# Two fused transformer blocks on one core: where the token's scale of the norm ahead of the experts is applied, and how a score's mask and maximum are formed

## The reference

```python
def rms_norm(x, g):
    y = x * lax.rsqrt(jnp.mean(x * x, axis=-1, keepdims=True) + EPS)
    return y * g

def peer(xn, peer_w_q, peer_sub_keys, peer_u, peer_v):
    qh = (xt @ peer_w_q).reshape(T, 8, 2, 128)                # queries
    sub = jnp.einsum("thpc,hpnc->thpn", qh, peer_sub_keys)    # against 2 x 128 keys a head
    v1, i1 = lax.top_k(sub[:, :, 0], 16)
    v2, i2 = lax.top_k(sub[:, :, 1], 16)
    cand = v1[..., :, None] + v2[..., None, :]                # 256 candidates a head
    vals, cidx = lax.top_k(cand, 16)
    gates = jax.nn.softmax(vals, axis=-1)
    # for the 16 experts of each head and token: h = xn . u, then gelu(h) * gate, then the sum with v
    ...

x = x + mixed @ w_out
x = x + peer(rms_norm(x, norm2_g), peer_w_q, peer_sub_keys, peer_u, peer_v)
```

## Time and profile before

| | us |
|---|---|
| median of 3 runs | 3203.68 (3203.49 to 3206.08) |
| the profiled execution | 3204.81 |
| its span | 3203.0 |
| TensorE busy in the span | 3185.0 |
| VectorE busy | 2226.0 |
| ScalarE busy | 1555.5 |

### The profile page before, as it was taken

How to read it: one execution, slowest core, us unless ns; L and a number is a source line. 1 busy time by engine, 2 the same in 40 slices (tenths; PEclk the granted TensorE clock), 3 DMA queues, 4 the chain that set the end, 5 groups by cost and what they waited for, 6 DMA issues and landing times.

```text
span 3203.0 us, 42378 instructions
## 1 busy us (share of the span) xinstructions
PE 3185.0 (99%) x17362; PEld 2707.6 (85%) x17362; DVE 2226.0 (69%) x3055; ACT 1555.5 (49%) x1998; POOL 13.7 (0%) x29
## 2 busy tenths in 40 slices
PE   9999999999999999999999999999999999999999
PEld 8888888888888888887888888888888788888887
DVE  6775556677577567766568997766687787865564
ACT  4564444555355455546544555455443344444353
POOL 0000000000000000000000000000000000000000
PEclk9999999999999999999999999999999999999999
DMA  7456665656665666653555666666666665556665
GB/s 252 154 162 218 211 211 180 210 191 191 191 190 190 193 188 192 205 170 111 190 154 171 217 216 189 188 183 224 190 190 212 203 200 173 188 184 192 194 184 171
DMA packets 175825, 610.61 MB, mean 191 GB/s; under 512 B 19201, under 2 KB 27553, under 8 KB 174736
## 3 DMA queue, kind: packets, MB, share of 16 engines
q1 hardware_dynamic: 173648, 599.93, 60.0%
q0 software_dynamic: 1984, 7.99, 0.8%
HBM read 597.36 MB, written 10.49 MB: 190 GB/s over the span
## 4 chain that ended last, share of the span: by engine, by line
PE 97%; DVE 2%; ACT 1%; issue 0%; DMA 0%; SPq 0%; ACTq 0%; DVEq 0%
PE PS L1194 29%; PE PS L1211 16%; PE PS L1213 16%; PE PS L1212 16%; PE PS L1191 15%; PE PS L1414 1%; PE PS L1427 1%; PE PS L1293 1%; DVE LO L1749 0%; PE PS L1247 0%; PE PS L1326 0%; ACT UN L1506 0%; ACT HI L1436 0%; PE PS L1305 0%; PE PS L1223 0%
## 5 line engine op out<-in xcount | busy, mean ns | idle before, releaser
L1749 DVE TENSOR_TENSOR LO<-RAW,HI 128x1024 fp32r<-128x1024 f32 (+1 forms) x1096 | 1325.1, 1218 | 698.0 <-ACT HI L1436 694.7
L1436 ACT ACTIVATE HI<-RAW 128x1024 fp32r<-128x1024 f32 (+1 forms) x1096 | 1148.3, 1054 | 1044.6 <-PE PS L1213 732.5
L1194 PE MATMUL PS<-XX,HI 128*128 128x512 f32 x4032 | 968.4, 391 | 0.0
L1194 PEld LDWEIGHTS PS<-XX,HI 128*128 128x128 f32 x4032 | 739.4, 188 | 145.1 <-issue 2.4
L1211 PE MATMUL PS<-HI,FH 128*128 128x512 f32 x1760 | 692.0, 393 | 1.7 <-DVE LO L1749 1.7
L1213 PE MATMUL PS<-HI,FL 128*128 128x512 f32 x1760 | 685.8, 390 | 0.0
L1212 PE MATMUL PS<-LO,FH 128*128 128x512 f32 x1760 | 684.7, 389 | 0.0
L1191 PEld LDWEIGHTS PS<-XX,LO 128*128 128x128 f32 x4032 | 520.2, 191 | 21.1 <-issue 1.0
L1191 PE MATMUL PS<-XX,LO 128*128 128x256 f32 x4032 | 536.8, 284 | 0.0
L1213 PEld LDWEIGHTS PS<-HI,FL 128*128 128x128 f32 x1760 | 330.3, 188 | 70.1
L1211 PEld LDWEIGHTS PS<-HI,FH 128*128 128x128 f32 x1760 | 330.3, 188 | 69.1 <-DVE LO L1749 2.2
(11 more groups left out here) (286 smaller groups left out, 1667.7 us busy)
## 6 DMA issues: line engine op xcount, KB each, us to landing
RAW<-in_peer_ut SPq DMA_DIRECT2D x256, 512.0 KB, 4.1
RAW<-in_peer_v SPq DMA_DIRECT2D x256, 512.0 KB, 4.2
RAW<-in_ffn_w_up SPq DMA_DIRECT2D x176, 512.0 KB, 4.2
RAW<-in_w_in SPq DMA_DIRECT2D x88, 512.0 KB, 4.3
RAW<-in_ffn_w_down SPq DMA_DIRECT2D x88, 512.0 KB, 4.2
RAW<-in_w_in_c SPq DMA_DIRECT2D x48, 512.0 KB, 3.7
RAW<-in_w_mix_out SPq DMA_DIRECT2D x32, 512.0 KB, 4.0
RAW<-in_w_in_2c SPq DMA_DIRECT2D x32, 512.0 KB, 3.7
```

Source lines behind the costliest of these rows:

```text
L1194: m = e.matmul(o, hi[:, k, x], XX[:, 4 * u + k, :, :].rearrange("p h s -> p (h s)"), start=first and k == 0, stop=last and k == 3, skip_gr ...
L1436: return e.activation(dst, src, ACT.Copy) if scale is None else e.activation(dst, src, ACT.Copy, scale=scale)
L1749: return e.tensor_tensor(dst, src, hi.bitcast(F32), ALU.subtract)
```

## The change

The norm ahead of the experts becomes a fourth turn of the kind described last: after each product of o2_last UN = RES * gain is formed and turned into XX without y1, in the steps of the next product. keep_busy(2), n2_mul and n2_turn are gone. The query reads these unscaled inputs, and the keys' results are scaled by y1 as ScalarE copies them to SUB. The experts' products need the scaled inputs: y1 is spread into a tile RS2 (two matmuls), and between the query's units xn(q) adds XH and XL of a quarter and multiplies with RS2 on VectorE, into the memory of UN. When the last query product has read a quarter, xn_split(q) copies it to XH (ScalarE) and forms XL (VectorE). The squares in o2_last go to another tile. In the attention each head's mask and maximum are one operation on VectorE.

The diff, cut to its core:

```diff
-    "att_score": (2, 0, 3),
+    "att_score": (2, 0, 4),
...
         emit("o2_last", g)
-    def turned_scaled(q):
...
-    keep_busy(2)
+        evacuations.append(turned(3, g))
+    advance(evacuations)
     emit("n2_sum")
-    emit("n2_mul", 0)
-    for _ in turned_scaled(0):
-        pass
-    for q in range(1, 4):
-        beside.append(turned_scaled(q))
+    def scaled_inputs():
+        yield from pause(2)
+        spread("n2_spread")
+        yield from pause(8)
+        for q in range(4):
+            emit("xn", q)
+            yield from pause(2)
+    beside.append(scaled_inputs())
...
-                product(("wq_both", g, i), 4)
+                product(("wq_both", g, i), 4, behind=(lambda u: emit("xn_split", u)) if (g, i) == (3, 1) else None)
...
             emit("mm", len(p.unit_of))
             p.unit_of.append((step_, u, u == 0, u == n - 1))
+            if behind is not None:
+                behind(u)
...
-            elif kind in ("wq", "wq_both", "us", "x"):
-                w.wait_ge(s_dve, V("n2_turn", j))
+            elif kind in ("wq", "wq_both"):
+                w.wait_ge(s_dve, V("turn", 3, j))
+            elif kind in ("us", "x"):
+                w.wait_ge(s_dve, V("xn_split", j))
...
-                    copy(SUB[:, t, 4 * g:4 * g + 4, :], four(spare(step, t))).then_inc(s_act, 1)
+                    copy(SUB[:, t, 4 * g:4 * g + 4, :], four(spare(step, t)), y1[:, t:t + 1]).then_inc(s_act, 1)
+            elif kind == "xn_split":
+                q, = k
+                w.wait_ge(s_mm, multiplied(("wq_both", 3, 1), q))
+                w.wait_ge(s_dve, V("xn", q))
+                copy(blocks(XH, q), blocks(GM[0], q)).then_inc(s_act, 1)
...
-                    e.activation(UN[:, t, c], RES[:, t, c], ACT.Square, accum_out=SSQ[:, t, g:g + 1]).then_inc(s_act, 1)
+                    e.activation(junk1[:, t, :], RES[:, t, c], ACT.Square, accum_out=SSQ[:, t, g:g + 1]).then_inc(s_act, 1)
...
-                    e.tensor_tensor(s4[:, 2 * g:2 * g + 2, r, 0:n],
-                                    spare(step, r)[:, 0:2 * n].rearrange("p (h k) -> p h k", k=n),
-                                    mask[:, 256 * qt:256 * qt + n].unsqueeze(1).to_broadcast([128, 2, n]),
-                                    ALU.add).then_inc(s_dve, 1)
-                w.wait_ge(s_dve, V(*step, k=2))
-                e.tensor_reduce(mx[:, 4 * g:4 * g + 4], sc[:, 4 * g:4 * g + 4, 0:n], AX.X, ALU.max).then_inc(s_dve, 1)
+                    for j in range(2):
+                        h = 4 * g + 2 * j + r
+                        e.tensor_tensor_reduce(sc[:, h, 0:n], spare(step, r)[:, n * j:n * j + n], mask[:, 256 * qt:256 * qt + n],
+                                               1.0, NEG, ALU.add, ALU.max, mx[:, h:h + 1]).then_inc(s_dve, 1)
...
+            elif kind == "xn":
+                q, = k
+                d = blocks(GM[0], q)
+                w.wait_ge(s_pe, P("turn", 3, 3))
+                w.wait_ge(s_dve, V("turn", 3, q))
+                w.wait_ge(s_act, A("n2_spread"))
+                e.tensor_tensor(d, blocks(XH, q).bitcast(F32), blocks(XL, q).bitcast(F32), ALU.add).then_inc(s_dve, 1)
+                w.wait_ge(s_dve, V("xn", q, k=1))
+                e.tensor_tensor(d, d, RS2[:].unsqueeze(1).to_broadcast([128, 4, S]), ALU.mult).then_inc(s_dve, 1)
+            elif kind == "xn_split":
+                q, = k
+                w.wait_ge(s_act, A("xn_split", q))
+                rest(blocks(XL, q), blocks(GM[0], q), blocks(XH, q)).then_inc(s_dve, 1)
```

More of the change, by code:

```diff
@@ L125 @@
     "ln_mean": (0, 2, 2), "ln_root": (0, 1, 5), "ln_norm": (0, 0, 1), "ln_turn": (2, 4, 0), "ln_out": (0, 1, 1),
-    "o2": (0, 0, 2), "o2_last": (0, 2, 2), "n2_sum": (0, 1, 6), "n2_mul": (0, 0, 2), "n2_turn": (2, 2, 2),
+    "o2": (0, 0, 2), "o2_last": (0, 2, 2), "n2_sum": (0, 1, 6), "n2_spread": (1, 3, 0), "xn": (0, 0, 2), "xn_split": (0, 1, 1),
     "wq": (0, 2, 0), "wq_both": (0, 1, 1), "keys": (2, 2, 0),
@@ L256, in plan, with product @@
     newest = [None]
-    def product(step_, n, halfway=None):
+    def product(step_, n, halfway=None, behind=None):
         pair = pairs[0] % 2
@@ L330, in score @@
             for r in range(2):
-                spare(me, r, (DVE_, me, r + 1))
+                spare(me, r, (DVE_, me, 2 * r + 2))
             emit(*me)
@@ L603, in plan @@
         emit("o2_last", g)
-    def turned_scaled(q):
[L606 to L612, removed]
-    keep_busy(2)
-    emit("n2_sum")
-    emit("n2_mul", 0)
-    for _ in turned_scaled(0):
-        pass
-    for q in range(1, 4):
-        beside.append(turned_scaled(q))
+        evacuations.append(turned(3, g))
+    advance(evacuations)
+    emit("n2_sum")
+    def scaled_inputs():
[6 more added lines that the diff above has]
+    beside.append(scaled_inputs())
     def choose(t, g):
@@ L883, in _program @@
     TK = over("TK", [128, 3, 384], 34 * K)
+    RS2 = over("RS2", [128, S], 33 * K)
     GM = [UN[:].rearrange("p t (k s) -> p (t k) s", s=S), over("GM1", [128, 16, S], 0)[:],
@@ L1238, in tensor @@
                 m.then_inc(s_pe, 1)
-            elif kind in ("turn", "n2_turn"):
+            elif kind == "turn":
                 q = k[-1]
                 for t in range(2):
-                    w.wait_ge(s_dve, V(*(("turn_mul", *k) if kind == "turn" else ("n2_mul", q)), k=t + 1))
+                    w.wait_ge(s_dve, V("turn_mul", *k, k=t + 1))
                     for s, n in until_free(step, t):
@@ L1258, in tensor @@
                     m.then_inc(s_pe, 1)
-            elif kind in ("first_spread", "ffn_spread"):
+            elif kind in ("first_spread", "ffn_spread", "n2_spread"):
                 w.wait_ge(s_act, A(kind, k=2))
@@ L1451, in scalar @@
                 e.activation(SM[:, 25:26], SM[:, 24:25], ACT.Sqrt).then_inc(s_act, 1)
-            elif kind in ("turn", "n2_turn"):
+            elif kind == "turn":
                 q = k[-1]
[L1454 to L1457, removed]
+                if k[0]:
+                    w.wait_ge(s_mm, multiplied({1: ("gt", 3), 2: ("f", 10, 1, 1), 3: ("h2", 3)}[k[0]]))
                 for t in range(2):
@@ L1479, in scalar @@
                     w.wait_ge(s_dve, V("first_sum"))
-                else:
-                    w.wait_ge(s_dve, V("ffn_sum"))
+                elif kind == "ffn_spread":
+                    w.wait_ge(s_dve, V("ffn_sum"))
+                else:
+                    w.wait_ge(s_dve, V("ln_out", 1))
+                    w.wait_ge(s_dve, V("n2_sum"))
                 for t in range(2):
@@ L1484, in scalar @@
                 w.wait_ge(s_pe, P(kind))
-                copy(RS[:], spare(step)[:, 0:S], 1024.0).then_inc(s_act, 1)
+                copy(RS2[:] if kind == "n2_spread" else RS[:], spare(step)[:, 0:S], 1024.0).then_inc(s_act, 1)
             elif kind == "kv":
@@ L1672, in scalar @@
                 c = slice(512 * g, 512 * g + 512)
-                w.wait_ge(s_pe, P("att_turn", 2, 1, 3))
+                w.wait_ge(s_dve, V("ln_out", 1))
                 for t in range(2):
                     w.wait_ge(s_dve, V("o2_last", g, k=t + 1))
-                    e.activation(UN[:, t, c], RES[:, t, c], ACT.Square, accum_out=SSQ[:, t, g:g + 1]).then_inc(s_act, 1)
+                    if g:
+                        w.wait_ge(s_act, A("o2_last", g - 1, k=t + 1))
+                    e.activation(junk1[:, t, :], RES[:, t, c], ACT.Square, accum_out=SSQ[:, t, g:g + 1]).then_inc(s_act, 1)
             elif kind == "wq":
@@ L1698, in scalar @@
                 blk, = k
-                w.wait_ge(s_pe, P("n2_turn", 3))
+                w.wait_ge(s_dve, V("xn_split", 3))
                 w.wait_ge(s_dve, V("gate", 1, 3))
@@ L1864, in vector @@
                     w.wait_ge(l_gq[g], 16)
+                elif s == 3:
+                    w.wait_ge(s_pe, P("att_turn", 2, 1, 3))
+                    w.wait_ge(l_gb2, 16)
+                    w.wait_ge(s_dve, V("o2_last", g))
                 elif s == 1:
```

6 lines of the change are left out of this document (3 added, 3 removed).

## The result

| | before | after |
|---|---|---|
| median, 16 runs each, us | 3204.27 (3203.22 to 3206.60) | 3209.99 (3208.02 to 3212.06) |
| profiled execution, us | 3204.81 | 3208.51 |
| its span, us | 3203.0 | 3206.7 |

The medians lie 5.7 us apart. The ratio, formed from all runs, is 1.0016, with an interval of 1.0009 to 1.0022: slower by 2.9 to 7.0 us. The interval leaves out no change at all, and the ratio itself is under the 0.2% that the forecast took for the least it could tell. The sixteen runs of the kernel before include the three of the first table. In the page TensorE is busy 3184.3 us, 0.7 less than in the earlier trace rows, and its span is 3.7 longer, so its idle time has grown by 4.4 us; what the low clock costs is inside the busy time.

The account below looks back on a forecast made before the run. TensorE, busy 3185.0 of 3203.0 us, was taken to bound the kernel. Gap -7.7, standstills +5.5 and +4.5, clock +4.2, attention -1.0 sum to +5.5, so 3209.2 us for the median, range 3201 to 3213.

Parts of the forecast that it names:

- The gap: TensorE's stretch between o2_last and the query, norm ahead of the experts: closing it gains 7.7 us net.
- keys(1): Group 1's keys product: TensorE stands still 5.5 us, three xn being ahead of the VectorE addition it needs.
- keys(2): Group 2's keys product: xn(3) adds 2.4 us on VectorE but is costed at nothing; uncovered 1 us.
- keys(3): Group 3's keys product: TensorE stands still 4.5 us, four xn_split being ahead of the VectorE addition it needs.
- The clock: TensorE's low clock after both standstills: loses 4.2 us, twice the mean of two priced wakes; bounds 0 and 5.2.
- The attention: Fused mask and maximum in the second attention's score steps: gains about 1.0 us; bounds 2.2 gain, 1 loss.
- bound on a head's price: Fused score operation on VectorE: at least 0.34 us per head for 256 keys, 0.21 for 128.
- The sum: Whole kernel: -7.7 + 5.5 + 4.5 + 4.2 - 1.0 = +5.5 us, median 3209.2.
- A: Rival, query stretch: VectorE hides the scaled inputs, no standstills; 3195.0 us, chance 0.13.
- B: Rival, attention scores: a fused head costs over 0.61 us for 256 keys, losing 1.0; 3211.2 us, chance 0.18.
- C: Rival, behind keys(1) and keys(3): standstills come but the clock stays up; 3205.0 us, chance 0.17.
- D: Rival, query start: a late split or bank leaves some 3 us of the gap; 3212 us, chance 0.05.

Follow-up runs that it names:

- xn_spaced: Changed kernel with three query units in place of two between the scaled inputs xn(q); 3207.13 us, ratio 1.0006 to the kernel before.
- xn_early: Changed kernel with the four scaled inputs xn(q) written seven units earlier, into the last units of wq; 3202.14 us, ratio 0.9991 to the kernel before.
- rests_behind: early_keys3 with xn_split of quarters 2 and 3 written behind the addition that keys(3) waits for; 3195.39 us, ratio 0.9969 to the kernel before.
- filled_half: Changed kernel with 22 and 18 useless identity matmuls ahead of keys(1) and keys(3); 3205.73 us, ratio 1.0000 to the kernel before.
- norm_only: Changed kernel with the score steps of before, so only the norm is changed; 3210.88 us, ratio 1.0016 to the kernel before.
- keys3_later: Changed kernel with only group 3's keys product moved back, by one unit in effect; 3205.31 us, ratio 0.9999 to the kernel before.
- early_keys3: xn_early with keys(3) one unit further back; 3197.35 us, ratio 0.9976 to the kernel before.
- keys_later: Changed kernel with the keys products of groups 1, 2 and 3 moved back, by one unit in effect; 3203.10 us, ratio 0.9995 to the kernel before.
- keys_two: Changed kernel with pause(4) ahead of the keys products of groups 1, 2 and 3, in effect keys_later's order; 3203.13 us, ratio 0.9995 to the kernel before.

## Why the prediction was right

- **The gap**: 7.7 us forecast, 7.6 measured. The transposes that moved into o2_last were costed at nothing beyond their own time. That holds in every trace with the new norm: no transpose waits there. (The wait on UN from VectorE's product that several lists hold, 1.3 us in xn_spaced, stands at 8 us, in the first norm, and the kernel before has it there too, with 0.50 us.)
- **keys(1)**: 5.5 forecast, 5.4 measured, and by the mechanism named: one pair less takes 2.38 off (xn_spaced), none leaves no wait (xn_early).
- **keys(2)**: nothing forecast, no wait.
- **keys(3)**: 4.5 forecast, 4.5 measured. The wait of 4.44 us is still there when the scaled inputs are early, and two rests less and one unit of room remove it (rests_behind), so it is theirs.
- **The clock**: 4.2 forecast as the mean of two wakes, 3.8 in the changed kernel's trace and 3.5 by filled_half's. That the mean of two wakes came this close is partly luck: behind waits of the same length the loss was 2.1 to 2.6 us at keys(1) (the changed kernel, norm_only, keys3_later) and 1.6 to 2.3 at keys(3) (the changed kernel, norm_only, xn_spaced, xn_early).
- **The attention** is the term that was mis-sized: 1.0 forecast, 1.8 in every trace with the fused operation, which is inside the bounds, and 2.6 in the changed kernel's own, where 0.8 of it is the shorter wake. The bound on a head's price was right: for 256 keys the fused operation is recorded with 0.42 us, but the heads follow each other at 0.34, the least that the text allowed. The steps of it in VectorE's timeline of the changed kernel:

```profile
1488.44 0.42 DVE L1949 CUSTOM_DVE_ANT_0 UN<-PS,CONST 128x256 f32<-128x256 f32 x1
1488.78 0.08 DVE L1949 DVE_READ_ACCUMULATOR2_ANT SM<- 128x1 f32 x1
1488.78 0.42 DVE L1949 CUSTOM_DVE_ANT_0 UN<-PS,CONST 128x256 f32<-128x256 f32 x1
```

What failed was the path: the prediction follows the score steps into the exponentials' chain alone. The product on UF stands behind them on VectorE too, and TensorE waited 0.8 us for it; the row was in the list of waits before and was not read as a consumer of the scores:

```profile
PE PS L1352 <- DVE UF L2172: 0.8, 1, 0.8
```

The length of the low clock behind UV changes from execution to execution with the same order; that the change shortens it is not shown. The Trainium skill (VectorE: DVE Perf Modes, section Two Vector instructions with no wait between them) has an accumulator output as two instructions. The trace agrees on the pair; the second one, 0.08 us, starts together with the next head and adds nothing to the 0.34 us from head to head, so the step down from the upper bound that was taken from ScalarE's pair wasn't there.

- **The sum**: +5.5 forecast; +3.7 between the two profiled executions, +5.7 between the medians. The profiled execution of after lies 1.5 us below its own median and that of before 0.5 above. Some 0.8 us of this is the short wake behind UV in the trace of after. The rest stays open; wakes of changing length behind keys(1) and keys(3) can make such a difference, but no trace of another execution of this kernel says so. That the forecast's 3209.2 lies 0.8 from 3210.0 is partly luck: the terms by the trace would have given 3207.4, and 3208.0 with 1.8 for the attention.

The rivals: the scaled inputs were not hidden where they were written (A), yet they could have been, as rests_behind shows; the fused operation wasn't dear (B); the clock didn't stay up (C); the gap closed (D).

## What to carry to other kernels

Work that is taken off one engine's path and put on another engine has a place in that engine's queue: find the first instruction behind it that the bounding engine waits for, and add up what is written between the last idle time and it. If the sum is more than the room, move the work to where the engine idles, or behind that instruction, before judging the idea; here the same edit was worth +5.7 us in one order and -10.4 in another. For the consumers of a shortened step, read every wait on that engine's later outputs, not only the chain that the step feeds.

## What the hardware showed that was not expected

Standstills of the same length did not always have the same consequence for the clock. After 1.64 and 1.65 us it stayed at 1.00 (keys3_later, early_keys3). After 2.41 us it stayed at 1.00 once, at keys(1), and fell to 0.50 once, at keys(3), in one and the same execution of keys_later; its windows behind the two waits:

```profile
1682.00:1684.00 2.00, 2.00 (x12) 1.70 (x11) 1.93 (x5) 1.80 (x3) 0.00 (x0) 1.00 0.25 102
...
1734.00:1736.00 2.00, 2.00 (x9) 1.71 (x8) 1.90 (x8) 1.12 (x3) 0.00 (x0) 0.50 0.79 240
```

keys_two, the same order in another execution, shows the same at both places (2.41 and 2.43 us), which speaks against mere chance; two executions don't settle it, and what differs between the two places no run shows. After 2.84, 3.40, 4.45 and 5.2 us it fell each time (xn_spaced, the wait on UV, and the changed kernel). Matmuls on the identity, which compute nothing that is used, kept it at 1.00 in filled_half, and 40 of them were worth 3.5 us there by the trace.
